# Eight channel tiles of a depthwise convolution on TensorE inside the product before it, with their transfers in ScalarE's queue

## The reference, cut to what matters

```python
def conformer_conv(h, w_pw1, b_pw1, w_dw, b_dw, ln_g, ln_b, w_pw2, b_pw2):
    u = h @ w_pw1 + b_pw1                       # 1024 -> 2048
    a, gate = jnp.split(u, 2, axis=-1)
    u = a * jax.nn.sigmoid(gate)
    u = lax.conv_general_dilated(u, w_dw[:, None, :], window_strides=(1,),
        padding=[(30, 0)], dimension_numbers=("NWC", "WIO", "NWC"),
        feature_group_count=1024) + b_dw        # causal, 31 taps, one filter a channel
    u = jax.nn.silu(layernorm(u, ln_g, ln_b))
    return u @ w_pw2 + b_pw2
```

## Time and profile before

| what | us |
|---|---|
| median of 3 runs (1307.89 to 1311.06) | 1310.67 |
| the profiled execution's own time | 1311.96 |
| its span, first to last instruction | 1310.6 |
| PE busy in the span | 1210.4 |
| DVE busy | 960.3 |
| ACT busy | 653.4 |
| mean granted clock of TensorE, share of full | 0.971 |

### The profile page before, as it was taken

The page is one execution under the profiler, slowest core; times in us unless marked ns, Lnnn a source line. Parts: engine busy times, 40 slices in busy tenths (PEclk is TensorE's granted clock), DMA queues, the critical chain, the costliest instruction groups (busy, mean ns, idle before and its releaser), DMA issues.

```text
span 1310.6 us, 24770 instructions
## 1 busy us (share of the span) xinstructions
PE 1210.4 (92%) x9796; PEld 1152.6 (88%) x9796; DVE 960.3 (73%) x1853; ACT 653.4 (50%) x1142; POOL 108.7 (8%) x106
## 2 busy tenths in 40 slices
PE   4978899999998999999978788999989879999999
PEld 4957899999987999999967678999989767999999
DVE  5966598878776888878886658888875555766653
ACT  5326554445446544445555664544444765545431
POOL 2001100002000200004000112000011112100000
PEclk9999899999999999999998989999999989999999
DMA  7487688877853678787633325887865422555552
GB/s 275 142 210 92 225 301 261 252 265 265 271 179 123 196 262 263 236 276 249 219 110 103 103 91 177 272 255 252 275 230 184 133 89 83 191 179 186 184 193 65
DMA packets 81126, 259.36 MB, mean 198 GB/s; under 512 B 8904, under 2 KB 20424, under 8 KB 81012
## 3 DMA queue, kind: packets, MB, share of 16 engines
q1 hardware_dynamic: 81012, 257.79, 62.1%
HBM read 252.68 MB, written 5.08 MB: 197 GB/s over the span
## 4 chain that ended last, share of the span: by engine, by line
PE 68%; DVE 18%; ACT 6%; issue 4%; DMA 1%; POOL 1%; DVEq 0%; ACTq 0%
PE ps L521 61%; DVE wlo L1188 6%; DVE aacc L1194 2%; DVE CV L1194 1%; PE ps L582 1%; DVE X L1194 1%; DMA raw<-wall 1%; ACT HH L840 1%; ACT oS L840 1%; PE ps L617 1%; ACT eS L840 1%; PE ps L613 1%; PE ps L612 1%; PE ps L621 1%; DVE tn L1191 1%
## 5 line engine op out<-in xcount | busy, mean ns | idle before, releaser
L521 PE MATMUL ps<-HH,whi 128*128 128x256 f32 (+1 forms) x2152 | 625.7, 291 | 32.9 <-DVE wlo L1188 13.9
L521 PE MATMUL ps<-HH,wlo 128*128 128x256 f32 (+1 forms) x2152 | 615.3, 286 | 0.0
L521 PE MATMUL ps<-HL,whi 128*128 128x256 f32 (+1 forms) x2152 | 615.0, 286 | 0.0
L840 ACT ACTIVATE whi<-raw 128x1024 fp32r<-128x1024 f32 x363 | 381.0, 1056 | 333.3 <-PE ps L521 328.0
L1188 DVE TENSOR_TENSOR wlo<-raw,whi 128x1024 fp32r<-128x1024 f32 x363 | 444.2, 1228 | 37.2 <-ACT whi L840 36.7
L521 PEld LDWEIGHTS ps<-HH,whi 128*128 128x128 f32 x2152 | 415.7, 193 | 51.7 <-issue 22.4
L521 PEld LDWEIGHTS ps<-HL,whi 128*128 128x128 f32 x2152 | 415.6, 193 | 0.4
L521 PEld LDWEIGHTS ps<-HH,wlo 128*128 128x128 f32 x2152 | 415.4, 193 | 0.0
L521 PE MATMUL ps<-GH,whi 128*128 128x256 f32 x704 | 198.2, 282 | 0.6 <-DVE bcol L1414 0.5
L521 PE MATMUL ps<-GL,whi 128*128 128x256 f32 x704 | 197.5, 281 | 0.0
L521 PE MATMUL ps<-GH,wlo 128*128 128x256 f32 x704 | 197.5, 280 | 0.0
(11 more groups left out here) (207 smaller groups left out, 984.7 us busy)
## 6 DMA issues: line engine op xcount, KB each, us to landing
raw<-wall SPq DMA_DIRECT2D x363, 512.0 KB, 4.3
araw<-ada SPq DMA_DIRECT2D x96, 512.0 KB, 4.7
UR<-uscr SPq DMA_DIRECT2D x24, 142.0 KB, 3.3
scratch<-bvec SPq DMA_DIRECT2D x1, 3072.0 KB
oBB<-kbias SPq DMA_DIRECT2D x16, 192.0 KB, 2.5
aTB<-scratch SPq DMA_DIRECT2D x12, 128.0 KB, 2.4
X<-x_in SPq DMA_DIRECT2D x2, 512.0 KB, 5.9
out<-X SPq DMA_DIRECT2D x8, 128.0 KB, 3.1
```

The source lines that it names most:

```text
L521: ins = pe.e.matmul(o, l, r, start=(kt == p.order[0] and i == 0), stop=(kt == p.order[-1] and i == 2))
L840: ac.then_inc(ac.e.activation(o, i, func, **kw), sem)
```

## The change

All eight channel tiles are summed on PE, DVE's 62 tap instructions go away, and the group for channel tile j runs inside the product: after tile 7 of pw1 group 0, after tile 9 group 1, and so on to group 4 after tile 15; groups 5 to 7 stay behind the product. Each group but the first is followed by the sum over the channels for the group before it, in bank 7. The writes to uscr, the reads into UR and the copy of the bias table to scratch are issued by ACT instead of SP. In ACT's loop over the tiles, a write (`taps_out`) stands at each even tile and the read of it (`taps_in`), with the wait for the landing, at the next odd tile; the copy to scratch stands at tile 4, ahead of the write of U's channel tile 1. DG has three buffers instead of six, and building it comes after U. Layer norm's HL is computed two steps behind the scaling instead of one.

```diff
-CONV_DVE = (0, 1)
-CONV_PE = tuple(j for j in range(KD) if j not in CONV_DVE)
+TAPS_AFTER = 6
...
 # PE
+                def taps(j):
+                    bk = bank[5 + j % 2]
+                    pe.wait_ge(S.dg, j + 1)
+                    pe.wait_ge(S.ur[j % 3], 64 * (j // 3 + 1))
+                    if j >= 2:
+                        pe.wait_ge(S.cva, j - 1)
+                    for m in range(8):
+                        for r in range(4):
+                            ins = pe.e.matmul(bk[32 * r:32 * r + 32, 0:T], DG[j % 3][:, 8 * r + m, :],
+                                              UR[j % 3][:, r, 4 * m:4 * m + T], start=(m == 0), stop=(m == 7))
+                    pe.then_inc(ins, S.cvt)
+                    if j:
+                        channel_sum(j - 1)
+
+                def channel_sum(j):
+                    pe.wait_ge(S.bv, 1)
+                    pe.wait_ge(S.cva, j + 1)
+                    return pe.e.matmul(bank[7][:, 0:T], ones[:, :], CV[:, j, :], start=(j == 0), stop=(j == KD - 1))
...
+                    j, odd_tile = divmod(nt - TAPS_AFTER, 2)
+                    if odd_tile and j >= 0:
+                        taps(j)
...
-                for n, j in enumerate(CONV_PE):
...
+                for j in range((16 - TAPS_AFTER) // 2, KD):
+                    taps(j)
+                pe.then_inc(channel_sum(KD - 1), S.lnt)
...
 # ACT
+                def taps_out(j):
+                    ac.wait_ge(S.u, j + 1)
+                    ac.wait_ge(S.uz, 2)
+                    load(uscr[j], U[:, j, :], S.uw[j % 3])
+
+                def taps_in(j):
+                    if j >= 3:
+                        ac.wait_ge(S.cvt, j - 2)
+                    ac.wait_ge(S.uw[j % 3], 16 * (j // 3 + 1))
+                    for c in range(4):
+                        src = bass.AP(uscr.tensor, uscr.offset + j * P * (31 + T) + c, [[31 + T, 32], [32 * (31 + T), 4], [1, UW]])
+                        load(UR[j % 3][32 * c:32 * c + 32, :, :], src, S.ur[j % 3])
...
                     if nt == 0:
                         norm_root(0)
+                    if nt == 4:
+                        ac.wait_ge(S.bv, 1)
+                        load(scratch, bvec[:, :].unsqueeze(1).broadcast_to([12, P, 512]), S.bd)
+                    if nt % 2 == 0 and nt:
+                        taps_out(nt // 2 - 1)
+                    if nt % 2 and nt > 1:
+                        taps_in(nt // 2 - 1)
                     if nt % 2 == 0:
                         ac.wait_ge(S.ev, slot_of("pw1", nt) + 1)
                         act(TMP[nt % 8][:, :], TMP[nt % 8][:, :], ACT.Sigmoid, S.sig, bias=V("bp1", 8 + nt // 2))
+                    j, odd_tile = divmod(nt - TAPS_AFTER, 2)
+                    if odd_tile and j >= 0:
+                        taps(j)
                 warm()
+                taps_out(KD - 1)
+                taps_in(KD - 1)
+                for j in range((16 - TAPS_AFTER) // 2, KD):
+                    taps(j)
...
 # DVE
-                    if nt >= 4:
-                        for _ in range(4):
-                            tap()
...
                         stt(U[:, n, 30:30 + T], t[:, :], V("bp1", n), TMP[(nt - 1) % 8][:, :], ALU.add, ALU.mult, S.u)
-                while taps:
-                    tap()
+                        dv.wait_ge(S.wq, 16)
+                        dv.wait_ge(S.id32, 3)
+                        if n >= 3:
+                            dv.wait_ge(S.cvt, n - 2)
+                        tt(DG[n % 3][:, :, :], id32[:, :].unsqueeze(1).broadcast_to([P, 32, 32]),
+                           wq[:, n, :].unsqueeze(2).broadcast_to([P, 32, 32]), ALU.mult, S.dg)
...
-                for kt in range(KD + 1):
+                for kt in range(KD + 2):
...
-                    if kt:
-                        dv.wait_ge(S.lnh, kt)
-                        tt(HL[LN_SET][:, kt - 1, 0:T], SQ8[:, kt - 1, :], HH[LN_SET][:, kt - 1, 0:T].bitcast(F32),
+                    if kt >= 2:
+                        dv.wait_ge(S.lnh, kt - 1)
+                        tt(HL[LN_SET][:, kt - 2, 0:T], SQ8[:, kt - 2, :], HH[LN_SET][:, kt - 2, 0:T].bitcast(F32),
                            ALU.subtract, S.lnl)
...
 # SP
-            for nt in range(17):
-                if nt < 16:
-                    lows(low_to("pw1", nt))
-                for n, j in enumerate(CONV_PE):
-                    if nt == 2 * j + 2:
-                        taps_out(n)
-                        if n < 3:
-                            taps_in(n)
-            for n in range(3, len(CONV_PE)):
-                taps_in(n)
-            sp.wait_ge(S.bv, 1)
-            load(scratch, bvec[:, :].unsqueeze(1).broadcast_to([12, P, 512]), S.bd)
+            rest("pw1")
             rest("pw2")
```

More of the change, by code:

```diff
@@ L333, in __init__ @@
         self.ara = [new(f"ara{i}") for i in range(ARAW)]
-        self.uw = [new(f"uw{i}") for i in range(len(CONV_PE))]
+        self.uw = [new(f"uw{i}") for i in range(3)]
         self.ur = [new(f"ur{i}") for i in range(3)]
@@ L352, in __init__ @@
         self.eps, self.id32, self.uz, self.dg, self.sig, self.u = new("eps"), new("id32"), new("uz"), new("dg"), new("sig"), new("u")
-        self.relm, self.bv, self.cvt, self.cva, self.cvd = new("relm"), new("bv"), new("cvt"), new("cva"), new("cvd")
+        self.relm, self.bv, self.cvt, self.cva = new("relm"), new("bv"), new("cvt"), new("cva")
         self.lnt, self.lnx, self.lnq, self.lnf, self.lns, self.lnh, self.lnl = (
@@ L410, in program @@
             CV = sb("CV", [P, KD, T], F32, st)
-            DG = {j: sb(f"DG{j}", [P, 32, 32], F32, st) for j in CONV_PE}
+            DG = [sb(f"DG{i}", [P, 32, 32], F32, st) for i in range(3)]
             UR = [sb(f"UR{i}", [P, 4, UW], F32, st) for i in range(3)]
@@ L840, in act, with load @@
                 ac.then_inc(ac.e.activation(o, i, func, **kw), sem)
+            def load(o, i, sem):
+                ac.then_inc(ac.e.dma_start(o, i), sem, 16)
             def highs(upto):
@@ L925, in convolution, with taps @@
             def convolution():
+                def taps_out(j):
[9 more added lines that the diff above has]
+                        load(UR[j % 3][32 * c:32 * c + 32, :, :], src, S.ur[j % 3])
+                def taps(j):
+                    ac.wait_ge(S.cvt, j + 1)
+                    act(CV[:, j, :], bank[5 + j % 2][:, 0:T], ACT.Identity, S.cva, bias=V("bdw", j))
                 for kt in range(KD):
@@ L938, in convolution @@
                         act(TMP[nt % 8][:, :], TMP[nt % 8][:, :], ACT.Sigmoid, S.sig, bias=V("bp1", 8 + nt // 2))
-                for n, j in enumerate(CONV_PE):
-                    ac.wait_ge(S.cvt, n + 1)
-                    act(CV[:, j, :], bank[5 + n % 2][:, 0:T], ACT.Identity, S.cva, bias=V("bdw", j))
+                    j, odd_tile = divmod(nt - TAPS_AFTER, 2)
+                    if odd_tile and j >= 0:
+                        taps(j)
                 warm()
+                taps_out(KD - 1)
+                taps_in(KD - 1)
+                for j in range((16 - TAPS_AFTER) // 2, KD):
+                    taps(j)
                 for kt in range(KD):
@@ L1307, in convolution @@
             def convolution():
[L1308 to L1318, removed]
                 dv.then_inc(dv.e.memset(epsb[:, :], EPS), S.eps)
@@ L1352, in convolution @@
                     if nt % 2:
[L1353 to L1358, removed]
                         dv.wait_ge(S.sig, n + 1)
@@ L2042 @@
     scratch = nc.dram_tensor("scratch", (12, P, 512), F32, kind="Internal").ap()
-    uscr = nc.dram_tensor("uscr", (len(CONV_PE), P, 31 + T), F32, kind="Internal").ap()
+    uscr = nc.dram_tensor("uscr", (KD, P, 31 + T), F32, kind="Internal").ap()
     out = nc.dram_tensor("out", (P, KD, T), F32, kind="ExternalOutput").ap()
```

## The result

The changed kernel takes 1341.69 us (median of 4 runs, 1335.93 to 1346.77) against 1310.74, the median of what are now four runs of the kernel before. The ratio is 1.024, with a 95% interval from 1.0195 to 1.0284: slower by 31 us, inside the forecast range. The profiled execution of the changed kernel is the fastest of its four: its span is 1334.6, against 1310.6.

The account below looks back on a forecast made before the run. PE was taken to bound the product. A hold behind the scratch copy (+45.6) less 5.3 back at gu0 gave +40.3: 1351 us from the median, 1352.3 from the profiled execution; range 1332 to 1368.

Parts of the forecast that it names:

- the hold: Product, tile 5: write of channel tile 1 waits behind scratch copy, stopping ACT, then PE; L +45.6 us, chance 0.83.
- L: Point where the channel sums end and layer norm starts: 101.8 us before, forecast at 147.4.
- the prediction's sums without a hold: L if no write waits behind the copy: 100.4, or 104.8 with the 4.4 of exposed hand-over.
- The hand-over of the last channel tile: After group 4, CV, write and reads delay group 7: 4.4 exposed, 1.1 to 7.1 by landings; taken as 6.
- A single channel sum: On PE after each group but the first: 0.46 each (3.67 / 8), eight sums 3.7.
- What came back: Start of gu0: with scratch long done, PE's stop behind the copy shrinks; 5.3 us back, 3 to 7.3.
- The long end of the hold's range: Copy shares DMA undiscounted, write lands at 101, UR at 107, hand-over 10, 3 given back: 1367 us.
- HL two steps behind: Layer norm: the third scaling fits into DVE's idle 0.63 before the first HL; nothing, at most 0.4 either way.
- The transfers' issue on ACT: ACT's product loop: 0.44 to 0.47 per issue, as SP's; round of 8 to 10.5 barely hidden by PE's 9.7.
- PE's gap would then end with a unit's split: Sign of being wrong: if weight loads stop with scratch too, a split instead of UR ends PE's gap.
- The first rival: ACT at tile 5: write not held, landing within about 15 us; -2.3, 1308 us (1302 to 1313), chance 0.10.
- 8.4 of waits and low clock: PE's path behind the product: removing DVE's taps saves waits of 4.34 and 2.24 and the low clock's 5.35 - 3.52.

Follow-up runs that it names:

- e2: Changed kernel with the whole copy to scratch moved behind the convolution's last read, still in ACT's queue: 1317.67 us, ratio 1.0045.
- e1: Changed kernel with half of the copy to scratch at tile 4 and half behind the convolution's last read: 1323.93 us, ratio 1.0103.
- e3: Kernel before with only the copy to scratch moved to ACT's queue, behind its last CV: 1320.27 us, ratio 1.0062.
- e5: Changed kernel with the copy to scratch issued by SP at tile 3 instead of by ACT: 1343.27 us, ratio 1.0242.
- e6: Changed kernel with the convolution's writes and reads issued by SP, the copy staying with ACT at tile 4: 1340.43 us, ratio 1.0224.
- e7: Changed kernel with the copy made via a small DRAM array, 128 copies outermost, still at tile 4: 1318.59 us, ratio 1.0054.
- e4: Changed kernel with the copy to scratch in eight pieces, one behind each channel tile's reads: 1330.35 us, ratio 1.0141.
- e9: Changed kernel with the copy made via a small DRAM array and placed behind the convolution's last read: 1308.01 us, ratio 0.9982.
- e8: Kernel before with the copy made via a small DRAM array, at its old place in SP's queue: 1310.17 us, ratio 0.9985.
- e10: As e9, but channel tiles 0 and 1 summed on DVE again, six groups on PE: 1305.55 us, ratio 0.9952.

## Why the prediction was right, point by point

**The bound, and the hold.** PE bounds the product: e2 has no PE wait in it, and its L of 102.4 lies between the 100.4 and the 104.8 of the prediction's sums without a hold. The hold was forecast at its place, with its release (the reads of group 1), and with the copy's length. From the issue of the held write to its landing I had 44.9 to 89, 44.1; it was 43.3.

**Sizes that were off.** The sum had L at 147.4; it was 135.9.

- The start of the hold. I had the copy issued at 44; it was at 37.75. The write of channel tile 0 landed after 2.1, not 5.3; it was issued at 33.76, where I had its source ready at 35; and the copy's issue did not stand behind the split of unit 9, which started at 37.73 and ran beside it. So PE resumed at 87.0, not 94: -7.0.
- The hand-over of the last channel tile: I took 6, and 1.1 for the shortest landings; it was 0. The groups 5 to 7 run back to back, 4.22 apart. The write's issue did not wait for the table load: the two started at 122.55 and 122.52. The last write, issued at 122.55, had landed by 124.96, after 2.4 instead of 5.3.
- A single channel sum costs 0.63 in the chain (4.22 for it and a group of 3.59), not 0.46, an eighth of the run of eight: 8 x 0.17 = +1.4. Together -7.0 - 6.0 + 1.4 = -11.6, against the 11.5 measured.
- What came back: 5.3 forecast, 4.6 measured between L and gu0. The median has +31.0, and the profiled execution +24.0 in its span; the stretch around the change accounts for 29.5. The rest, -5.5 in that execution, lies behind this stretch, in stages that no part of the change touches. The distance to the same sum of the kernel before is 29.5 at first, and at the later sums of the same kind 27.8 (446 us), 26.7 (1010) and 24.0 (1126). The last 2.7 fall in the last attention stage, where the granted clock was 0.82 from 1080 to 1100 in the execution of before and 0.99 in the matching stretch of the changed kernel. What sets the clock there stays open, and so do the other 2.8; the other three runs are 5 to 11 us longer than the profiled one.
- The long end of the hold's range was added up wrongly: its terms give L at 164.4 and 1370 us, not 1367. The measured time is far from it.

**The terms at nothing.** HL two steps behind: PE's wait ahead of pw2 is 4.32 before and in e1, e2 and the changed kernel. The transfers' issue on ACT: 0.44 each, as SP's.

**The step that was argued wrongly.** I read the weight loads' 15.1 of before as order inside a queue, and took it that SP's loads would not be held in the changed kernel. They were, for 19.6 to 23.2. The prediction had said that PE's gap would then end with a unit's split; it ended with UR all the same, because ACT, held longer, was last. In e3, e5 and e6 too, transfers in the other queue are held: weight loads for some 20 us, and the write for 23.1 and 21.3, half of the 43.3 in the copy's own queue. The forecast came out because in the changed kernel both effects point the same way, and that is luck. e5 is the case where they don't: by queue order I gave it 1320 to 1335, and it took 1343. The Trainium skill, DMA: Bandwidth & Descriptors, "Queues, rings and completion order", has the queues of an engine take turns at packet granularity. Here a 144 KB write in the other queue landed after 23.1 (e5), where the one before the copy took 1.9, so if they take turns, then at long intervals; no row here shows how long. Its "Issuing engines are not separate DMA queues", by which all transfers run on the same engines, fits the times better: with the copy or the convolution's transfers issued by SP or by ACT, they are 1340 to 1343.

**The first rival's threshold** (a write that lands within 15) was too lax: e7 shows a cost of 9 us (PE's wait of 6.2 and a group that takes 2.8 longer) with a landing of 16.0, its rows leave room for about 10, and e4 shows that 6.3 to 9.0 in every round is too much.

**Where the change's own gain went.** Sparing DVE its taps removes 8.4 of waits and low clock. Two more groups cost 7.0, single sums 1.4. That is 0, and e2's L says the same: 102.4 against 101.8. So do the times with the cured copy, 0.9982 with the change (e9) and 0.9985 without it (e8). e10 keeps the interleaving and gives DVE its two channel tiles back, and only then is there a gain.

## What to carry to other kernels

Here the long transfer held both queues, so its length and its form come before its queue and its place: look at the DMA share and rate of its stretch (0.69 and 78 GB/s here), and reshape it first (337 GB/s). An engine that does work for others should not wait for landings, and what it issues should not stand behind a transfer that is longer than its lead. Moving work from DVE to PE, the engine that bounds, gained nothing here even though it removed waits of PE: the 8.4 us that it removed were paid for in full. And a cure that is open to both kernels (here the copy's form) has to be in both before the change is judged.

## What the runs showed of the hardware that I had not expected

- An issue can block. Behind the copy, in its own queue, the write kept ACT for 18.42 us in the issue itself, and in e5 SP's second weight load took 14.49. Behind half of the copy (e1) the same write's issue took 0.35. In the other queue, most issues beside the copy took 2.8 to 5.1 instead of 0.33 to 0.45 (SP's weight loads in e3 and e6, SP's write and reads in e6, ACT's in e5).
- A copy from 12 partitions of SBUF, with 12 as its outermost dimension, moves 78 GB/s at a share of 0.69 of the engines, and the same 3 MB from DRAM to DRAM with 128 outermost 337 GB/s at a share of 1.0. The two edits were not run apart. The Trainium skill, DMA: Bandwidth & Descriptors, in "Why a DMA increments its semaphore by 16 and not by 1", has the number of engines follow from the outermost dimension; 12 of 16 is 0.75, near the trace's 0.69. The remaining factor of about 3 an engine (78 / 12 against 337 / 16) may lie in the source, SBUF or DRAM; no run shows which.
- A group of 32 matmuls behind an idle stretch of PE of 6 us and more took 5.0 to 6.5 instead of 3.66 (the changed kernel, e1, e5, e6, e7). In the changed kernel the granted clock is 0.71 from 87 to 92, behind 32.5 us of idle, and 1.00 after that, so part of the stretch is at the lower level of 1.2 GHz; in e7, behind 6.2 us, it is 0.56 for 6.5 us.
